# A new table of step durations for the list scheduler of a two-block hybrid transformer kernel

## The reference: what is computed

```
x = first_block(x, ...)      # per layer: one input projection, then three causal attentions, gate, w_out, layer norm
x = second_block(x, ctx...)  # per layer: rms norm with modulation, one input projection, then three branches
...
# block 1, layer: 128 queries at a time
#   diff: 4 heads x 2 maps, softmax(q1 k1) - lam * softmax(q2 k2), values of width 128
#   dsa:  4 heads, keys chosen by the top 64 of an index score (8 heads, relu, weighted sum)
#   fox:  4 heads, with a cumulated log forget gate added to the scores
#   mixed = concat(a, b, c) * silu(gate);  x = layer_norm(ALPHA * x + mixed @ w_out)
# block 2, layer: x and a context of 256 tokens
#   conv: 31 taps depthwise, layer norm, silu;  gla: gated linear attention, both directions
#   attention: 8 query heads, 2 key heads, rms-normed and rotated
#   x += gate * (sigmoid(g0)*conv@w + sigmoid(g1)*gla@w + sigmoid(g2)*att@w) @ w_out
```

## Time and profile before

| what | value |
|---|---|
| median of three runs | 1391.77 us (1391.14, 1391.77, 1396.12) |
| span of the profiled execution, first to last instruction | 1390.8 us |
| PE busy | 1315.5 us, 95% |
| DVE busy | 875.9 us, 63% |
| ACT busy | 585.0 us, 42% |
| POOL busy | 282.2 us, 20% |
| mean granted TensorE clock | 0.974 |

### The profile page before, as it was taken

One profiled execution on the slowest core, in us unless ns is written; L12 is line 12 of the kernel. 1 busy time (PEld: TensorE's weight loads), 2 busy tenths in 40 slices (PEclk: granted clock), 3 DMA queues, 4 the chain that ended last, 5 costly groups with the idle time before them and its releaser, 6 DMA issues.

```text
span 1390.8 us, 18894 instructions
## 1 busy us (share of the span) xinstructions
PE 1315.5 (95%) x7490; PEld 1037.9 (75%) x7490; DVE 875.9 (63%) x1496; ACT 585.0 (42%) x968; POOL 282.2 (20%) x217
## 2 busy tenths in 40 slices
PE   7999987999979899997999999999999999889998
PEld 5777776777757777776777777777788876578876
DVE  4795756685677543488997542333686688855654
ACT  3444533444454445222434442332573554336542
POOL 0110013110033322247000011211342132201122
PEclk9999998999999999998999999999999999989999
DMA  7674465363433411112111122323553332204453
GB/s 251 230 270 140 142 243 191 132 222 137 162 111 95 156 62 61 46 61 76 47 60 46 61 64 94 100 91 91 167 174 99 98 119 82 71 31 137 151 175 99
DMA packets 49193, 168.47 MB, mean 121 GB/s; under 512 B 5863, under 2 KB 7079, under 8 KB 48849
## 3 DMA queue, kind: packets, MB, share of 16 engines
q1 hardware_dynamic: 49104, 167.26, 36.6%
HBM read 166.19 MB, written 1.05 MB: 120 GB/s over the span
## 4 chain that ended last, share of the span: by engine, by line
PE 74%; DVE 10%; issue 9%; POOL 5%; ACT 1%; DMA 1%; SPq 0%; POOLq 0%; ACTq 0%; DVEq 0%
PE bank L1528 16%; PE bank L1529 15%; PE bank L1530 15%; PE bank L1447 3%; PE bank L1841 3%; DVE conv_val L2597 3%; PE bank L1546 3%; PE bank L1547 2%; PE bank L1548 2%; DVE w_lo L2277 2%; PE bank L1608 2%; PE bank L1816 2%; PE bank L1571 1%; PE bank L1461 1%; PE bank L1759 1%
## 5 line engine op out<-in xcount | busy, mean ns | idle before, releaser
L1528 PE MATMUL bank<-w_hi,x_hi 128*128 128x512 f32 (+4 forms) x1120 | 466.9, 417 | 15.7 <-DVE x_lo L2287 9.9
L2277 DVE TENSOR_TENSOR w_lo<-w_raw,w_hi 128x1024 fp32r<-128x1024 f32 (+3 forms) x264 | 322.7, 1225 | 241.5 <-ACT w_hi L1878 241.2
L1878 ACT ACTIVATE w_hi<-w_raw 128x1024 fp32r<-128x1024 f32 (+3 forms) x264 | 269.9, 1027 | 424.8 <-PE bank L1530 258.4
L1529 PE MATMUL bank<-w_lo,x_hi 128*128 128x512 f32 (+4 forms) x1120 | 437.1, 390 | 0.0
L1530 PE MATMUL bank<-w_hi,x_lo 128*128 128x512 f32 (+4 forms) x1120 | 436.3, 390 | 0.0
L1528 PEld LDWEIGHTS bank<-w_hi,x_hi 128*128 128x128 f32 x1120 | 216.2, 193 | 70.3 <-DVE x_lo L2287 12.1
L1530 PEld LDWEIGHTS bank<-w_hi,x_lo 128*128 128x128 f32 x1120 | 214.4, 191 | 46.6
L1529 PEld LDWEIGHTS bank<-w_lo,x_hi 128*128 128x128 f32 x1120 | 215.6, 192 | 38.9
L2597 DVE SCALAR_TENSOR_TENSOR conv_val<-conv_u,par,conv_val 128x512 f32<-128x512 f32 (+1 forms) x240 | 148.5, 668 | 0.0
L2915 POOL TENSOR_TENSOR merged<-merged,sigma 128x512 f32<-128x512 f32 x24 | 38.3, 1625 | 166.4 <-DVE sigma L2639 166.4
L1546 PE MATMUL bank<-x_hi,w_hi 128*128 128x512 f32 (+1 forms) x192 | 67.0, 349 | 0.5 <-ACT conv_val L2080 0.5
(11 more groups left out here) (342 smaller groups left out, 1790.2 us busy)
## 6 DMA issues: line engine op xcount, KB each, us to landing
w_raw<-in_w SPq DMA_DIRECT2D x172, 512.0 KB, 3.5
w_raw<-in_wm SPq DMA_DIRECT2D x48, 512.0 KB, 5.2
w_raw<-in_wo SPq DMA_DIRECT2D x40, 512.0 KB, 3.5
w_raw<-in_wy_gla SPq DMA_DIRECT2D x8, 512.0 KB, 3.6
w_raw<-in_wy_att SPq DMA_DIRECT2D x8, 512.0 KB, 3.5
w_raw<-in_wy_conv SPq DMA_DIRECT2D x8, 512.0 KB, 3.5
w_raw<-in_w SPq DMA_DIRECT2D x8, 460.0 KB, 5.4
w_raw<-in_w SPq DMA_DIRECT2D x12, 288.0 KB, 2.8
```

The lines of the kernel that those rows point to most:

```text
L1528: mm(out, xh[:, q, col], hi[:, kk, 0:w], start=kp == 0 and kk == 0 and not with_bias, stop=False)
L1529: mm(out, xh[:, q, col], lo[:, kk, 0:w], start=False, stop=False)
L1878: do(hi, raw, ACT.Copy).then_inc(sem["cut_hi"], 1)
L2277: v.tensor_tensor(lo, raw, hi.bitcast(F32), ALU.subtract).then_inc(sem["cut_lo"], 1)
```

## The change

Only numbers that `Plan.length` returns are changed. No instruction is added or taken away; what the program computes is the same, and the order of steps is worked out anew from the new numbers. `att_s` and `index_s` get durations of their own, by kind (dsa, diff, fox, index) and by query tile (1.65 times as long for the second). 63 entries of `LENGTH` change, `project` of 512 columns goes from 1.36 to 1.40. `SLACK`, `NOTICE`, `TRANSFER`, `rank` and `POOLS` stay.

```
-            return 1.36 * max(width, 64) / WC + (0.22 if kind in ("in2", "in2c") and kp == 0 else 0.0)
+            return 1.4 * max(width, 64) / WC + (0.22 if kind in ("in2", "in2c") and kp == 0 else 0.0)
...
+        if step[0] in ("att_s", "index_s"):
+            return {"dsa": 1.0, "diff": 0.9, "fox": 0.8}.get(step[2], 0.5) * (1.0 if step[3 if step[0] == "att_s" else 2] == 0 else 1.65)
```

More of the change, by code:

```diff
@@ L572, in length @@
             width = 32 if kind in ("in2", "in2c") and c == LRQ and t not in tiles_of(l) else columns_of((kind, l, c))
-            return 1.36 * max(width, 64) / WC + (0.22 if kind in ("in2", "in2c") and kp == 0 else 0.0)
+            return 1.4 * max(width, 64) / WC + (0.22 if kind in ("in2", "in2c") and kp == 0 else 0.0)
         if step[0] == "project_t":
-            return 1.36 if step[1] == 0 else 0.72
+            return 1.4 if step[1] == 0 else 0.72
         if step[0] in ("cut_hi", "cut_lo"):
             return LENGTH[step[0]] * columns_of(self.pieces[step[1]]) / WC
+        if step[0] in ("att_s", "index_s"):
+            return {"dsa": 1.0, "diff": 0.9, "fox": 0.8}.get(step[2], 0.5) * (1.0 if step[3 if step[0] == "att_s" else 2] == 0 else 1.65)
         return LENGTH.get(step[0], 0.1)
@@ L703 @@
 LENGTH = {
[L704 to L708, removed]
@@ L709 @@
-    "index_relu": 0.45, "att_exp": 1.0, "att_t_act": 0.4, "att_out_diff": 0.48, "fox_e": 2.0, "gate_silu": 0.45, "mi_sq": 1.1,
-    "mi_act": 1.4, "mi_hi": 0.55, "bias_sel": 1.4, "ev2": 0.48, "ev_val": 0.57, "ev_glu": 0.57, "ev_cg": 0.57, "ev_sig": 0.48,
-    "ev_gate": 0.48, "conv_sq": 0.52, "conv_sd": 0.5, "conv_silu": 0.75, "conv_hi": 0.52, "lr_t": 0.48, "gla_e": 2.6,
-    "gla_e3": 0.6, "gla_dec": 0.2, "gla_e12": 1.0, "gla_qt": 0.48, "gla_o1": 0.3, "aq_act": 0.48, "a_exp": 0.72, "a_t_act": 0.48,
@@ L713 @@
[L713 to L722, removed]
@@ L723 @@
-    "mi_add": 1.0, "u_zero": 1.95, "conv_u": 1.25, "conv_g": 1.25, "acc_add": 1.25, "gated": 1.25, "gla_zero": 2.2, "gla_ks": 1.25,
-    "gla_ki": 1.25, "gla_cp": 1.85, "gla_sq": 1.25, "gla_iv": 2.3, "hr_sq": 1.25, "hr_iv": 2.3, "hr_add": 1.25, "out_add": 1.25}
+    "load": 2.0, "mod": 0.5, "mod_t": 0.25, "flip": 0.45, "heads": 0.42, "att_v": 0.5, "fox_c": 0.6, "mi_flip": 0.43,
+    "conv_mean": 3, "conv_var": 2.7, "lr_flip": 0.43, "gla_z": 1.05, "gla_left": 1, "gla_tot": 0.9, "gla_cum": 1,
+    "gla_qf": 0.43, "gla_kf": 0.43, "gla_a": 0.86, "gla_con": 0.42, "gla_o": 4.8, "ak_flip": 0.43, "aq_flip": 0.43, "a_s": 1.1,
@@ new lines @@
+    "a_flip": 0.43, "a_v": 0.92, "gate_ones": 0.25,
+    "cut_hi": 1.03, "mod_row": 0.21, "mod_col": 0.15, "lam_exp": 0.2, "flip_hi": 0.5, "ev1": 0.48, "heads_act": 0.48,
+    "index_relu": 0.45, "att_exp": 1.0, "att_t_act": 0.4, "att_out_diff": 0.48, "fox_e": 2.0, "gate_silu": 0.45, "mi_sq": 1.1,
+    "mi_act": 1.4, "mi_hi": 0.55, "bias_sel": 1.4, "ev2": 0.48, "ev_val": 0.57, "ev_glu": 0.57, "ev_cg": 0.57, "ev_sig": 0.57,
+    "ev_gate": 0.56, "conv_sq": 0.52, "conv_sd": 0.5, "conv_silu": 0.75, "conv_hi": 0.52, "lr_t": 0.59, "gla_e": 3.15,
@@ new lines @@
+    "gla_e3": 0.56, "gla_dec": 0.2, "gla_e12": 1.0, "gla_qt": 0.6, "gla_o1": 0.38, "aq_act": 0.48, "a_exp": 0.75, "a_t_act": 0.48,
+    "gate_rows": 0.58,
+    "cut_lo": 1.22, "flip_lo": 0.6, "lam_dots": 0.57, "lam": 0.4, "rope": 1.3, "ev_fv": 0.33, "heads_dve": 0.6, "index_iw": 0.1,
+    "index_w": 0.96, "index_top": 0.75, "index_sel": 0.2, "att_max": 0.5, "att_norm": 0.6, "att_t_dve": 0.5, "att_out": 0.34,
+    "sub_sum": 0.7, "sub_end": 1, "fox_z": 1.1, "fox_l": 0.1, "fox_cum": 0.1, "fox_cols": 0.2, "gate_mul": 0.49, "resid": 1.3,
@@ new lines @@
+    "ln_stat": 0.25, "ln_x": 0.75, "ln_dve": 2, "bias_zero": 1.1, "bias0": 4.5, "scale": 0.55, "mi_ms": 0.1, "mi_x": 0.8,
+    "mi_dve": 0.6, "mi_lo": 0.78, "tap": 0.62, "conv_dev": 0.5, "conv_ve": 0.6, "conv_rs": 2.56, "conv_n": 0.5, "conv_lo": 0.9,
+    "ev_y": 0.64, "gla_one": 0.54, "gla_la": 0.6, "gla_qi": 0.89, "gla_kt": 0.6, "gla_m": 0.6, "gla_st": 0.55, "gla_o2": 0.33,
+    "gla_ms": 0.75, "gla_n": 0.86, "hr_ms": 0.6, "hr_n": 1.31, "ak_t": 0.6, "aq_dve": 0.6, "a_max": 0.63, "a_inv": 0.1,
@@ L726 @@
+    "a_t_dve": 0.6, "att_out2": 0.6, "gate_diag": 0.45, "out_gate": 0.6,
+    "roped": 1.67, "sub_sq": 1.25, "sub_pow": 2.8, "ln_pow": 0.46, "ln_pool": 3.24, "mean_w": 0.2, "bias1": 4.5, "mi_pow": 0.71,
+    "mi_add": 1.32, "u_zero": 1.95, "conv_u": 1.25, "conv_g": 1.25, "acc_add": 1.6, "gated": 1.39, "gla_zero": 2.8, "gla_ks": 1.58,
+    "gla_ki": 1.67, "gla_cp": 0.84, "gla_sq": 1.12, "gla_iv": 2.3, "hr_sq": 0.84, "hr_iv": 2.47, "hr_add": 1.37, "out_add": 1.75}
 TABLE = {"lam_exp": "exp", "att_exp": "exp", "gla_e3": "exp", "gla_dec": "exp", "gla_e12": "exp", "a_exp": "exp",
```

## The result

The changed kernel took 1416.4 us (median of 4 runs, 1413.0 to 1423.1), the kernel before 1393.9 beside it: ratio 1.0175, 95% interval 1.0147 to 1.0203. It is slower: by 22.4 us if the two medians are subtracted, by 24 if the ratio is taken. 1383.5 was forecast, and 1404 was the high end. What is read from it is therefore the loss of a bad execution, larger than the typical one.

The account below looks back on a forecast made before the run. PE, busy 95% of the span, was taken as the bound, with 111 us idle or at half speed to win. Gains of 12 less 2 for lost cover and 2 for block 2 gave 8 us: 1383.5, range 1365 to 1404.

Parts of the forecast that it names:

- The last attention: Block 2's end, 1150 to 1232 us: no wait named that must close, so 0 taken, bounds -10 and +10.
- Attention of block 1 packed tighter: Truer score lengths end block 1's attention sooner against projections, closing late waits: 12 us gain; as rival 1, chance 0.41.
- Lost cover: Block 1's full stretches: transposes and values placed too early wait for DVE or ACT; 2 us loss, bounds 0 and 26.
- Block 2's wait: Layer 0, 646 us: pooled numbers put the transpose too early, wait for `gated` grows 1 to 2 us; 2 us loss.
- Case 3: Rival: transposes and values of 32 maps in block 1 each wait for DVE or ACT; 1404 us, chance 0.16.
- case 4: Rival: block 2's layer 0, taps slowed beside POOL and query chain understated, waits for `gated` grow; 1400 us, chance 0.12.

Follow-up runs that it names:

- e5: The changed kernel with new numbers for block 2's steps only, old ones for block 1's: 1410.6 us, 18.7 us slower than before.
- f1: The kernel before with the new numbers in layer 1 of block 1 alone: 7.6 us faster than before.
- h2: The kernel before with the new numbers in layer 0 of block 1 alone: 17 us slower by the ratio.
- h1: e5 with heads' norm numbers held apart for key and query heads, and taps and conv steps by layer: 1371.1 us.
- k4: e5 with taps and conv steps by layer only, the heads' norm still pooled: 6 us faster than e5.
- k3: e5 with only the heads' norm numbers held apart for key and query heads: 20 us faster than e5.
- e4: The kernel before with the new numbers for block 1's steps alone: 5.5 us slower; ten runs from 1393.9 to 1406.0 us.
- k6: The changed kernel with heads' norm numbers by key and query, taps and conv steps by layer: 1381.5 us.
- f3: e5 with three projections of the last input chunk held back between the last gla_con steps: 1408.3 us.
- g1: The kernel before with every table number multiplied by its own random factor within 2%: 0.7% slower than before.
- g2: The kernel before with every table number multiplied by its own random factor within 2%, another seed: 1.1% slower than before.
- f2: e5, same order, with 16 matmuls of 512 columns, results overwritten, added in the last attention: 5 us slower than e5.
- k2: h1 with every number of block 2's table multiplied by its own random factor within 2%: 1373.6 us.

## Why the prediction was wrong, step by step

The largest failure is the last attention, which was taken at nothing. Under it lies a premise: that before's order is a typical one for its table, so that a truer table can only mend it.

**The last attention, 0 (bounds -10 and +10).** The step that failed: +11.7, and +11.8 in e5, which has block 2's new numbers alone. No wait was named that must close, and the middle was taken. 3.9 us of it are idle time and 10.3 clock. What in the new numbers makes it is not settled. Two redraws of before's table cost E 9.3 and 7.2 us. Before's own order lost 3.7 there in f1 and h2, by the clock. Numbers by shape turn the loss into a gain (E 226.4 in h1), but neither group of them does alone: taps and conv steps by layer alone leave it at 251.8 (k4), the heads' norm alone at 239.6 (k3).

**Attention of block 1 packed tighter, -12.** Right in layer 1 by its sum, where 6 + 2 + 1 were taken: L1 is 6.9 us shorter in the changed kernel and 10.6 in f1. The link from packing to waits was weaker than forecast. Diff's values came 14 projection steps sooner, but the waits on `x_lo` fell from 8.9 to 7.0 and 6.3, not under 5, and the clock gave f1 more than the idle time did. In layer 0, where 2 + 1 were taken, there was no gain, though diff's last values moved even further there: from behind the last input projection to 20 steps before it.

**Lost cover, +2 (bounds 0 and 26).** Mis-sized. L0 is 20.4 us longer, by 8.6 more idle and 17.3 more of clock. e4, with the same order, was 8.9 us shorter there by its clock alone, so 11 us are the steadier part of it (e4 11.5, h2 11.0). The place was wrong as well. Transposes and values, which had been priced, hardly wait. The next heads' transposes, the first scores and `fox_c` do, 5.3 us for copies out of PSUM.

**Block 2's wait, +2 (bounds -13.8 and +6).** The sum lay at its bound, +6.0, but not by the wait that was named. The wait for `gated` was to grow by 1 to 2 us and fell by 1.7. A wait of 3.9 for a weight piece's low part, cut by DVE, came in its place. That the numbers by shape matter here was right: h1's M is 14.1 us shorter than before's, of which 3.3 come back in the stretch behind it, and 13.8 had been put on it.

**Sum.** -6.9 + 20.4 + 6.0 + 11.7 - 0.3 elsewhere is the 30.9 of the profiled execution, against -8. The median lies 6.7 us lower. The prediction counted a microsecond at half speed as half of the work; `gla_o`'s matmuls show 1.8 times the time, so its clock terms are a tenth too high, which changes no sign. Without block 1's new numbers (e5) 18.7 us are left, without block 2's (e4) 5.5.

**The rivals.** Case 3 and case 4 ended on the right side. Case 3's price per wait is refuted. Of case 4 the part on pooled shapes is supported, though as a gain that was missed, not as the new loss. Its other part, that durations hang on DVE's and POOL's company, is not needed for a gain, since constants by shape win 22 us. The Trainium skill, SBUF — State Buffer, section "Who interferes with whom", was weighed there as speaking against any table of means; no run here tells its share apart.

**What was left out** is that two tables with no less truth in them, 2% off, cost 10 and 15 us. A case of its own for "any redraw of this order loses about 0.9%" would have moved the forecast to the slower side. It is also why the cause of the loss against before stays partly open: e5's 18.7 us are little more than such a redraw.

## What to carry to other kernels

Before refining a list scheduler's table, hold apart the shapes of one kind of step: here that was worth 35 and 40 us (k6 against after, h1 against e5), and 63 refined entries without it cost 22. Test a new table with noise on it: if 2% moves the time by more than the gain, what is measured is the draw of an order. Where such noise makes each draw slower, as both did here, the old order is likely a lucky one, and a truer table starts with that handicap.

## What the runs showed of the hardware

TensorE's granted clock did not follow from the instruction order alone. The same order gave 0.95 and 0.71 in 40 to 75 us. Over the second `gla_o` it gave the full 2.4 GHz in before and 1.2 GHz from 1194.7 us on in f1, behind the same waits of 0.8, 0.5 and 0.7 us. Being busy did not bring the clock back at once: over `gla_o` and the small matmuls behind it PE stayed at 1.2 GHz for 17.1 us in k3 (busy 16.45), 23.9 in f3 (22.73), 27.3 in f1 (24.23) and 41.0 in g1 (35.98) and g2 (34.74). In f2 eight matmuls of 512 columns among them didn't end it. h1 and k2, without waits there, kept 2.4 GHz over both `gla_o` in their profiles. What lets the clock fall in one execution and not in the other stays open.

At 1.2 GHz the same group of `gla_o`'s matmuls took 2.20 us, against 1.23 at 2.4 GHz, 1.8 times and not twice as long.
